# Seven-product units: VectorE's rest moved from four pieces ahead to three, and joins put first in each step

## The reference

```python
def swiglu(x, w_gu, w_down):
    g, u = jnp.split(x @ w_gu, 2, axis=-1)
    return (jax.nn.silu(g) * u) @ w_down          # d_ff = 2816 = 22 columns of 128

h = h + swiglu(rms_norm(h, ffn_norm[layer]), ffn_w_gu[layer], ffn_w_down[layer])   # layer 0 and 1
```

## Time and profile before

| what | value |
|---|---|
| median of 3 runs | 2273.27 us (2273.06 to 2274.67) |
| the profiled execution | 2274.58 us, span 2272.8 us |
| PE busy | 2173.3 us, 96% |
| DVE busy | 1468.4 us, 65% |
| ACT busy | 1081.6 us, 48% |
| mean granted PE clock | 0.986 |

### The profile page before, as it was taken

One profiled execution on the slowest core, in us unless ns is written; L12 is line 12 of the kernel. 1 busy time (PEld: TensorE's weight loads), 2 busy tenths in 40 slices (PEclk: granted clock), 3 DMA queues, 4 the chain that ended last, 5 costly groups with the idle time before them and its releaser, 6 DMA issues.

```text
span 2272.8 us, 33448 instructions
## 1 busy us (share of the span) xinstructions
PE 2173.3 (96%) x12698; PEld 1858.4 (82%) x12698; DVE 1468.4 (65%) x2344; ACT 1081.6 (48%) x1700; POOL 320.8 (14%) x267
## 2 busy tenths in 40 slices
PE   8999999998989999999989889999999999999998
PEld 6788887888978978877879889877788778888887
DVE  6666666578888853465688878656765756555522
ACT  5445545344444434565444454445665564444312
POOL 0212222400000030002300000120111125222211
PEclk9999999998999999999989999999999999999999
DMA  3311111121222232211212222332212214222221
GB/s 140 115 49 56 38 39 55 56 93 60 103 80 93 94 111 77 91 37 38 93 57 92 94 75 99 124 130 75 70 38 89 70 38 141 100 92 92 95 105 60
DMA packets 31675, 185.00 MB, mean 81 GB/s; under 512 B 3104, under 2 KB 7712, under 8 KB 11312
## 3 DMA queue, kind: packets, MB, share of 16 engines
q1 hardware_dynamic: 29520, 175.48, 22.4%
q0 software_dynamic: 2016, 7.60, 1.0%
HBM read 178.84 MB, written 7.37 MB: 82 GB/s over the span
## 4 chain that ended last, share of the span: by engine, by line
PE 68%; DVE 17%; ACT 8%; issue 6%; DMA 0%; SPq 0%; DVEq 0%; POOL 0%; ACTq 0%; POOLq 0%
PE ps L2328 18%; PE ps L2330 17%; PE ps L2329 17%; DVE wl L1480 4%; ACT wh L655 3%; PE ps L2654 2%; PE ps L3145 1%; ACT wh L523 1%; PE ps L3088 1%; PE ps L3128 1%; PE ps L2648 1%; DVE wsum L1451 1%; DVE hT L1517 1%; DVE raw L1464 1%; DVE raw L1458 1%
## 5 line engine op out<-in xcount | busy, mean ns | idle before, releaser
L2328 PE MATMUL ps<-xh,wh 128*128 128x512 f32 (+1 forms) x1616 | 613.0, 379 | 18.4 <-ACT scaled L672 14.6
L2330 PE MATMUL ps<-xh,wl 128*128 128x512 f32 (+1 forms) x1616 | 585.4, 362 | 0.0
L2329 PE MATMUL ps<-xl,wh 128*128 128x512 f32 (+1 forms) x1616 | 584.5, 362 | 0.0
L2328 PEld LDWEIGHTS ps<-xh,wh 128*128 128x128 f32 x1616 | 308.1, 191 | 70.2 <-ACT wh L655 17.1
L2330 PEld LDWEIGHTS ps<-xh,wl 128*128 128x128 f32 x1616 | 306.8, 190 | 48.2
L2329 PEld LDWEIGHTS ps<-xl,wh 128*128 128x128 f32 x1616 | 308.0, 191 | 42.5 <-issue 4.3
L1226 DVE TENSOR_TENSOR wl<-raw,wh 128x2048 fp32r<-128x2048 f32 x92 | 212.9, 2314 | 175.6 <-ACT wh L523 175.4
L523 ACT ACTIVATE wh<-raw 128x2048 fp32r<-128x2048 f32 x92 | 175.8, 1911 | 161.2 <-PE ps L2330 160.9
L2328 PE MATMUL ps<-part_h,wh 128*128 128x256 f32 (+1 forms) x672 | 222.8, 331 | 10.8 <-DVE hT L1517 8.7
L2330 PE MATMUL ps<-part_h,wl 128*128 128x256 f32 (+1 forms) x672 | 220.2, 328 | 0.0
L2329 PE MATMUL ps<-part_l,wh 128*128 128x256 f32 (+1 forms) x672 | 219.8, 327 | 0.0
(11 more groups left out here) (427 smaller groups left out, 4118.3 us busy)
## 6 DMA issues: line engine op xcount, KB each, us to landing
raw<-in_stream SPq DMA_DIRECT2D x158, 1024.0 KB, 4.8
hankd<-tabd SPq DMA_DIRECT2D x1, 3072.0 KB, 17.0
hank<-hankd POOLq DMA_DIRECT2D x4, 768.0 KB, 5.0
hT<-in_xT SPq DMA_DIRECT2D x4, 512.0 KB, 6.5
keepd<-hT POOLq DMA_DIRECT2D x1, 2048.0 KB, 10.1
hT<-keepd POOLq DMA_DIRECT2D x8, 256.0 KB, 4.8
out<-hT SPq DMA_DIRECT2D x8, 256.0 KB, 2.5
raw<-in_stream SPq DMA_DIRECT2D x2, 512.0 KB, 8.4
```

The lines of the kernel that those rows point to most:

```text
L2328: pe.matmul(out, w_hi, a_hi, start=start, stop=False, skip_group_check=goes_on)
L2329: pe.matmul(out, w_hi, a_lo, start=False, stop=False, skip_group_check=goes_on)
L2330: return pe.matmul(out, w_lo, a_hi, start=False, stop=stop, skip_group_check=goes_on)
```

## The change

In every step p of the seven-product loop:

- ACT: `copy_out` of piece p-1 and `silu` stand ahead of `hi` of piece p+4. Before, `hi` stood first.
- DVE: `lo` is done for piece p+3 instead of p+4 (`LO_LEAD`), so its rounding was made by ACT one step earlier. The join or add of piece p-1 stands ahead of `lo` and `sums`. Before, it stood behind both.
- Start: `lo` of three pieces, not four, stands ahead of the last plain column.

No instruction is added or removed.

```diff
+LO_LEAD = 3
@@ ACT products()
                     for p in range(len(ORDER) + 4):
-                        if p + LEAD < len(ORDER):
-                            hi(*ORDER[p + LEAD])
-                        elif p < len(ORDER):
-                            down_hi(p + LEAD - len(ORDER))
                         j, k = ORDER[p - 1] if 0 < p <= len(ORDER) else (None, None)
                         if j in GATES and k in (0, 2, 4):
                             copy_out(j, k)
...
                             silu(STREAM[j][1])
+                        if p + LEAD < len(ORDER):
+                            hi(*ORDER[p + LEAD])
+                        elif p < len(ORDER):
+                            down_hi(p + LEAD - len(ORDER))
@@ DVE products()
                     for p in range(len(ORDER) + 5):
-                        if p + LEAD < len(ORDER):
-                            lo(*ORDER[p + LEAD])
-                        elif p < len(ORDER):
-                            down_lo(p + LEAD - len(ORDER))
-                        if p + LEAD + 1 < len(ORDER):
-                            sums(*ORDER[p + LEAD + 1])
                         j, k = ORDER[p - 1] if 0 < p <= len(ORDER) else (None, None)
                         if j not in GATES and j is not None:
                             add_half(j, k)
...
                             gate_right(j)
+                        if p + LO_LEAD < len(ORDER):
+                            lo(*ORDER[p + LO_LEAD])
+                        elif p + LO_LEAD < len(ORDER) + 4:
+                            down_lo(p + LO_LEAD - len(ORDER))
+                        if p + LEAD + 1 < len(ORDER):
+                            sums(*ORDER[p + LEAD + 1])
@@ DVE, ahead of the loop
-                for p in ORDER[:LEAD]:
+                for p in ORDER[:LO_LEAD]:
                     lo(*p)
```

## The result

The changed kernel takes 2213.4 us (median of 4 runs, 2211.08 to 2215.02) against 2273.66 us before (4 runs): a ratio of 0.9734, 95% interval 0.9717 to 0.9751, 60.3 us less. The forecast was 2201 us with a range of 2180 to 2224: right in direction, inside the range, and 12 us too optimistic. The span falls from 2272.8 to 2211.5 us. Lines of the changed file are one higher than in the text above.

A forecast was written before the change was run, and what follows sets the result against it. The prediction took the DVE-ACT ring to hold the kernel above PE's pace; window savings of 6.2 + 3.3 + 3.0 + 17.1 + 3.0 + 3.5 = 36.1 us per stage, 72.2 in all, gave 2201 us, range 2180 to 2224.

The forecast's parts named there:

- The ring: Gate units: DVE sums, ACT rounds, DVE subtracts, each idle while the other works; 2.0 us per unit, said to go.
- The load loop: Gate units: rest of piece 6, load, rounding, next rest of a piece 6; 9.9 us, 11.4 with pair sums.
- DVE's wait for `wh`: Sign to check in each stage: DVE's waiting for ACT's roundings falls from 45 us to under 8.
- Pair work: Gates 10 to 17: two gate units with a pair take 22.0 us against PE's 19.9, 2.1 lost per pair.
- a landing 1 us later: Upper bound for gate units: 4.0 us of stall per pair, also stalls without pairs, 8 us more per stage.
- Down units: Four down units, twice per stage: from 42.8 to 39.8 us each time, 9.9 us per unit.
- Start and end: In ffn0, first 15 pieces from 34.5 to 28.3 us, last 27 pieces from 42.2 to 38.7.
- Rival 1: DVE keeps up everywhere, no load or pair stall, the start cured: 2178 to 2188 us; chance 0.12.
- Rival 2: Load or pair work holds `lo` in most units, stalls over 2 us return: 2235 us, 2222 to 2265; chance 0.14.
- Rival 3: Slower: joins first make DVE wait for PE, so the two take turns; 2297 us; chance 0.03.
- Rival 4: No change within 0.2% (4.5 us), PE being held by something the order doesn't touch; chance 0.03.
- The rule on DVE's pipe: Skill's rule that DVE's next operation starts on an empty pipe; would cost 15 us of gain; prediction kept 0.60 us.

The follow-up runs named there:

- piece 6 early: The changed kernel with the rest of piece 6 made right behind that of piece 5, ahead of the first sums and pair sums: 2207.8 us.

## Why the prediction was right, and where it was off

- **The ring goes.** Right, and shown: the lead of three alone gives it all. What the prediction added to it, that the copies go first "so PE gets them at the end of the product", carries nothing here by itself and costs 36 us without the lead. I had not priced the edits one by one.
- **The load loop.** Right in mechanism and size: 5.68 us from rest to rest (5.8 said), 11.36 us round with pair sums (11.4 said). Half a load takes 18.7 us off the time, so the loop costs something. A two-unit turn with a pair was forecast at 22.0 us and took 22.52.
- **DVE's wait for `wh`.** Said to fall from 45 us to under 8 per stage. It fell to 16.0 in ffn0: one wait in each of 16 units, 0.42 to 2.66 us, on the rest of piece 0 behind a landing. My own loop says as much: 9.9 us round against 8.4 of DVE's work leaves 1.5 us of waiting in a gate unit. The sum had the loop, and the sign did not.
- **Pair work.** The term "2.1 us lost per pair" was too small. It left out DVE's 0.51 us wait for the pair roundings. It also counted DVE's work only, not ACT's: the four roundings stand ahead of the copy and of the next `hi`. Gates 10 to 17 came out 2.1 us over the forecast in ffn0, three pairs of it; with the roundings a step later and piece 6 early 20.4 us went, 14.7 of them with the roundings.
- **Landings.** I took every landing as 4.8 us. Some take longer. Two neighbouring loads in the chain of ffn1, and what stands behind the second on ACT and PE:

```profile
1232.23 4.79 DMA raw<-in_stream
1242.14 5.98 DMA raw<-in_stream
```

```profile
1248.15 0.63 ACT L656 ACTIVATE wh<-raw 128x512 fp32r<-128x512 f32 x1 [2.90 <-DMA raw<-in_stream]
1248.68 0.37 ACT L673 ACTIVATE fork<-ps 128x256 f32<-128x256 f32 x1
```

```profile
1249.19 0.36 PE L2329 MATMUL ps<-t_h,wh 128*128 128x256 f32 x1 [0.80 <-ACT fork L673]
```

  The copy that PE needs was ready to be made, and stood behind the `hi` that waited for the load. So the cover of three pieces does not hold for it: a late landing reaches PE through the copy at once. This is 1.0 us here. What ffn1 lost more than ffn0 (90.2 against 88.6, 40.4 against 38.6) has three such stalls, 0.80, 0.26 and 0.85 us, each behind a load of 5.4 to 6.0 us. I named "a landing 1 us later" as a bound and left it out of the sum.
- **Down units.** 40.5 instead of 39.8 for four. It is one stall at the second unit, 0.58 us in its row, so 0.82 by the rows above:

```profile
570.74 0.35 PE L2329 MATMUL ps<-part_h,wh 128*128 128x256 f32 x1 [0.58 <-DVE hT L1518]
```

- **Start and end.** 27.7 against 28.3, and 38.6 against 38.7 in ffn0: right. The first stall came out at 2.32 us with slow matmuls behind it, the second as 0.98 and 0.26. But the parts that I named for the start (1.1, and 5 less 1.5) make only 4.6 us of the 6.2 that I took. Slow matmuls behind the first stall ran from 516.77 to 522.67 before and from 515.38 to 518.50 after, which was in no part. Gates 8 and 9 were 2.0 us worse in ffn0: 1.1 of it is a copy behind a `hi` that waited 2.95 us for a landing, as above, which ffn1 does not have (0.9 worse).
- **The sum.** The two stages fell short by 4.8 and 6.9 us, 11.7 of the 12 that the forecast was off. The terms that were too small are in the main the pair work and the late landings; the down units add 0.7 in each run of four.
- **Rivals.** Rival 1 (2178 to 2188) fell with the load loop. Rival 2 fell: no idle time over 2 us is left in gates 10 to 17, and the clock is 1.00. Rival 3 fell: the joins first alone make the kernel 12 us faster, not slower. Rival 4 fell with the result. The line at 2 us, which I drew for slow matmuls, is not sharp: before, they follow idle times of 2.15 to 3.52 us in ffn0, but not those of 2.35 (623.73) and 2.79 (650.94); none follow a shorter one.
- **The rule on DVE's pipe.** Rests start 0.60 us apart in the changed kernel too. The section of the Trainium skill that I set against this (VectorE: DVE Perf Modes, The DRAIN you can't avoid) also says that a next operation that is not held starts earlier, which I left out. The rows fit that sentence, so they are not at odds with the page.

Open: what makes single landings 1 us longer was not tried.

## What to carry to other kernels

Where two engines hand a piece to and fro, put one step between the hand-overs first: here that alone gave the whole 60 us. Reordering inside the step, with the hand-over still in it, gave 12 us (joins first) or cost 36 (copies first), and once the step was there it gave nothing that these runs can tell. When that ring is gone, look for the next loop through a buffer (here rest, load, rounding, rest) and add it up before trusting the busy shares; and check each sign you name against that sum. Short bursts on a half idle engine, such as four roundings of 1.9 us on one that is 49% busy, hold what stands behind them: look at what is queued there, not at the share.

## What was unexpected of the hardware

- Two-input operations on POOL and DVE at the same time: POOL's 128x512 rest took 1.75 us (1.1 by itself, as estimated above), DVE's 1.46 to 1.78 instead of 0.69, with both inputs in SBUF. With one input in PSUM DVE was not slowed (0.41).
- A PE stall cost 0.24 us more than the idle time in its row (1.38 us start to start instead of 0.12 at an idle time of 1.11, and 0.20 instead of 0.12 behind it).
- Transfers of the same 1 MB took 4.76 to 5.98 us in the chain of the two stages.
